# Sample tokens of the linear-attention layer: answers in four column tiles, state updates from values spread through DRAM

## The reference, cut to what matters

```python
def gla_chunk_step(S, inp):
    q, k, v, g = inp
    ...
    o = jnp.einsum('bhij,bjhv->bihv', attn, v) + jnp.einsum('bihk,bhkv->bihv', q * jnp.exp(bcum), S)
    b_last = bcum[:, -1]
    k_dec = k * jnp.exp(b_last[:, None] - bcum)
    S = jnp.exp(b_last)[..., None] * S + jnp.einsum('bjhk,bjhv->bhkv', k_dec, v)
    return S, o
```

## Time and profile before

| | |
|---|---|
| median of 3 runs | 1551.72 us (1551.42 to 1552.45) |
| the profiled execution | 1551.42 us, span 1549.7 us |
| TensorE busy | 1447.2 us (93%) |
| VectorE busy | 1175.9 us (76%) |
| ScalarE busy | 822.4 us (53%) |
| GpSimd busy | 248.7 us (16%) |
| mean granted TensorE clock | 0.981 |
| DMA | 243.11 MB, mean 157 GB/s |
| step 0 of heads 0, 1, 2, 3 | near 84 to 109, 173 to 194, 247 to 266 and 329 to 359 us |

### The profile page before, as it was taken

The page is one execution under the profiler, slowest core; times in us unless marked ns, Lnnn a source line. Parts: engine busy times, 40 slices in busy tenths (PEclk is TensorE's granted clock), DMA queues, the critical chain, the costliest instruction groups (busy, mean ns, idle before and its releaser), DMA issues. The chain is left out here.

```text
span 1549.7 us, 31393 instructions
## 1 busy us (share of the span) xinstructions
PE 1447.2 (93%) x11610; PEld 1195.0 (77%) x11610; DVE 1175.9 (76%) x2595; ACT 822.4 (53%) x1837; POOL 248.7 (16%) x438
## 2 busy tenths in 40 slices
PE   6999999799999979899999999989999999999985
PEld 5979787666788858898888888767787777777754
DVE  4555587856786887968977898986879787587775
ACT  4735353446465544546655765653657364655451
POOL 5010113101231200012111112120003110000012
PEclk8999999999999999999999999999999999999998
DMA  6455455335476542547854764843585664554541
GB/s 190 132 155 148 129 168 151 112 114 171 120 205 191 160 122 71 150 122 182 253 145 121 237 191 140 240 140 94 167 247 143 189 183 144 175 150 150 175 137 61
DMA packets 283778, 243.11 MB, mean 157 GB/s; under 512 B 32856, under 2 KB 251036, under 8 KB 283468
## 3 DMA queue, kind: packets, MB, share of 16 engines
q1 hardware_dynamic: 273708, 208.28, 45.6%
q0 software_dynamic: 9920, 32.84, 7.9%
HBM read 180.40 MB, written 64.97 MB: 158 GB/s over the span
## 5 line engine op out<-in xcount | busy, mean ns | idle before, releaser
L1447 PE MATMUL bank<-h,w 128*128 128x268 f32 (+1 forms) x4752 | 835.3, 330 | 22.5 <-ACT w L857 15.8
L1447 PEld LDWEIGHTS bank<-h,w 128*128 128x128 f32 x4752 | 699.4, 191 | 102.1 <-issue 28.4
L873 DVE TENSOR_TENSOR w<-w_raw,w 128x1024 fp32r<-128x1024 f32 x132 | 160.9, 1219 | 35.5 <-ACT w L857 34.9
L842 PE MATMUL bank<-s_w_out,s_yt_hi 128*128 128x512 f32 (+2 forms) x544 | 169.8, 402 | 3.8 <-DVE s_ys L2532 3.8
L857 ACT ACTIVATE w<-w_raw 128x1024 fp32r<-128x1024 f32 x132 | 138.7, 1051 | 8.1 <-DMA w_raw<-in_ssd_w_in_dram 8.1
L1525 DVE SCALAR_TENSOR_TENSOR conv<-before_conv,cw,conv 128x260 f32<-128x260 f32 (+2 forms) x216 | 125.3, 580 | 4.2
L842 PEld LDWEIGHTS bank<-s_w_out,s_yt_hi 128*128 128x128 f32 (+2 forms) x544 | 97.1, 182 | 30.8 <-issue 4.4
L842 PE MATMUL bank<-g_w_out,g_ot_hi 128*128 128x512 f32 (+2 forms) x288 | 97.0, 426 | 1.6 <-DVE g_ot_lo L2073 1.3
L842 PE MATMUL bank<-s_w_out,s_yt_lo 128*128 128x512 f32 x240 | 95.6, 398 | 0.0
L2616 ACT ACTIVATE s_yt_hi<-bank 128x512 fp32r<-128x512 f32 (+1 forms) x36 | 20.1, 557 | 126.5 <-PE bank L2607 126.4
L2319 ACT ACTIVATE s_decay<-s_decay,t_ac 128x128 f32<-128x128 f32 (+1 forms) x288 | 85.4, 379 | 1.2
(11 more groups left out here) (256 smaller groups left out, 2503.4 us busy)
## 6 DMA issues: line engine op xcount, KB each, us to landing
w_raw<-in_ssd_w_in_dram SPq DMA_DIRECT2D x80, 512.0 KB, 4.3
w_raw<-in_gla_w_in_dram SPq DMA_DIRECT2D x48, 512.0 KB, 4.3
s_decay<-kept_acd SPq DMA_DIRECT2D x32, 512.0 KB, 6.2
w_raw<-in_ssd_w_out_dram SPq DMA_DIRECT2D x30, 512.0 KB, 4.0
g_chunk<-kept_gq SPq DMA_DIRECT2D x32, 448.0 KB, 4.9
s_chunk<-kept_sq SPq DMA_DIRECT2D x32, 384.0 KB, 4.8
kept_sq<-stage SPq DMA_DIRECT2D x80, 134.0 KB, 4.3
kept_sq<-stage SPq DMA_DIRECT2D x40, 256.0 KB, 4.7
```

Source lines behind the costliest of these rows:

```text
L842: last = pe.matmul(bank[0:r, :], yt[a][:, k, 0:r], wo[:, b, 512 * half:512 * half + 512], start=(k + a + b == 0), stop=(k == tiles - 1 and ...
L873: dve.tensor_tensor(self.part(i, 1), self.raw(i), hi, ALU.subtract).then_inc(self.w_lo, 1)
L1447: last = pe.matmul(bank[:, 0:n], w[:, p.tile % 2, a, k, :], h[:, b, k, c:c + n], start=(i == 0), stop=(i == len(terms) - 1))
```

## The change

The answers: `g_q_masked` gets 32 columns per sample, and each answer product writes one column tile, 32 partitions of the second half of bank `O`, with sample c in tile c mod 4. Tasks 0 and 2 do nothing on TensorE, ScalarE and VectorE; task 1 handles four samples and task 3 the other four, each with four products. ScalarE copies the bank's half to `g_answers`, and one product with a stack of four identities (`g_near_masks`, last slot) adds the four tiles into the step's output, ahead of the attention's own product.

The new states: SP stores the 8 rows of values to DRAM (`store_values`, behind ScalarE's turned values) and loads them back spread over all 128 partitions, 1 MB (`load_values`, behind a wait for the store's landing). ScalarE scales each state by its decay in place, behind its answer, and VectorE adds value times key. The outer products, `g_k_masked` and VectorE's `dve_keys` go; ScalarE turns the meta tokens' keys with a scale that clears the samples' rows. GpSimd's task stays as it was, four times a head. Some semaphores of the size computation are merged.

```diff
         gla = [("distance", 1), ("keys", 0), ("levels", 0), ("decay", 1), ("turn", -1), ("fill", 0.5), ("load", 2),
...
-               ("fill", 0.5), ("lows",), ("fill", 0.5), ("weight", 1, 0), ("r_square", -1), ("r_out", -2),
-               ("fill", 0.5), ("lows",)]
+               ("fill", 0.5), ("lows",), ("fill", 0.5), ("v_out", 1), ("weight", 1, 0), ("r_square", -1), ("r_out", -2),
+               ("fill", 0.5), ("lows",), ("v_in", 1)]
...
-                 (0, ("scale", 0))]
+                 (0, ("scale", 0)), (0, ("v_out", 0)), (0, ("v_in", 0))]
...
-                            for i in range(4):
+                            for i in (1, 3):
+                                tasks.append(("sample", L, u, i - 1))
                                 tasks.append(("sample", L, u, i))
-                                tasks.append(("fill", at[0]))
+                                tasks.append(("fill", 2 * at[0]))
...
+    def store_values(self, sp, u):
+        e = ev(u, 0)
+        sp.wait_ge(self.vr_turned, e + 1)
+        sp.dma_start(self.d["v_rows"][u], self.t["vr"][0:NS, e % 2, 0:HV]).then_inc(self.v_moved, 16)
+
+    def load_values(self, sp, u):
+        sp.wait_ge(self.v_moved, 32 * u + 16)
+        if u:
+            sp.wait_ge(self.ss_new, NS * u)
+        sp.dma_start(self.t["vb"][:, :, :], self.d["v_rows"][u].unsqueeze(0).to_broadcast([P, NS, HV])).then_inc(
+            self.v_moved, 16)
...
+        for q in (4 * u + i - 1, 4 * u + i):
+            pe.wait_ge(self.ss_in[q % SAMPLES], 16 * (q // SAMPLES + 1))
+        for j in range(4):
+            c = 2 * (i - 1) + j
+            last = pe.matmul(self.O[SUB * j:SUB * (j + 1), HV:2 * HV], t["qm"][:, c * SUB:(c + 1) * SUB],
+                             t["ss"][:, (4 * u + c // 2) % SAMPLES, c % 2, :], start=(i == 1), stop=(i == 3))
         last.then_inc(self.ss_prod, 1)
...
+    def act_sample(self, act, u, i):
+        t, e = self.t, ev(u, 0)
+        if i % 2 == 0:
+            return
+        act.wait_ge(self.ss_prod, 2 * u + i // 2 + 1)
+        if i == 3:
+            act.activation(t["part"][:, :], self.O[:, HV:2 * HV], ACT.Copy).then_inc(self.ss_kept, 1)
+        for q in (i - 1, i):
+            for b in range(2):
+                st = t["ss"][:, (4 * u + q) % SAMPLES, b, :]
+                last = act.activation(st, st, ACT.Copy, scale=t["eb"][:, e % 2, 2 * q + b:2 * q + b + 1])
+            last.then_inc(self.ss_kept, 1)
...
+        dve.wait_ge(self.v_moved, 32 * (u + 1))
+        dve.wait_ge(self.k_ready0, 2 * (u + 1))
+        for q in (i - 1, i):
+            dve.wait_ge(self.ss_kept, self.kept_count(u, q))
+            for b in range(2):
+                c, st = 2 * q + b, t["ss"][:, (4 * u + q) % SAMPLES, b, :]
+                dve.scalar_tensor_tensor(out=st, in0=t["vb"][:, c, :], scalar=t["kd0"][:, c:c + 1], in1=st,
+                                         op0=ALU.mult, op1=ALU.add).then_inc(self.ss_new, 1)
...
+        if s == 0:
+            pe.wait_ge(self.ss_kept, 5 * u + 3)
+            pe.matmul(self.O[0:n, 0:HV], self.t["near"][:, 5, 0:n], self.t["part"][:, :], start=True, stop=False)
```

More of the change, by code:

```diff
@@ L559, in _ @@
                 ssd.load_first_z(sp, *at)
+            elif name == "v_out":
+                gla.store_values(sp, *at)
+            elif name == "v_in":
+                gla.load_values(sp, *at)
         gla.all_saved(sp)
@@ L617, in _ @@
                 ssd.act_inputs(act, *at[1:])
-            elif name == "sample" and at[0] == 1:
-                ssd.act_sample(act, *at[1:])
+            elif name == "sample":
+                layers[at[0]].act_sample(act, *at[1:])
             elif name == "square":
@@ L1704, in prepare @@
         t, consts = self.t, self.consts
-        mask, mask0, rowsel = t["mask"], t["mask0"], t["rowsel"]
+        mask, mask0, late = t["mask"], t["mask0"], t["late"]
         for li, h in enumerate(gla_levels(1)[0]):
@@ L1708, in prepare @@
         pool.memset(mask0[:, :, :], 0.0).then_inc(consts, 1)
-        pool.memset(rowsel[:, NS:NS + 1], 1.0).then_inc(consts, 1)
-        pool.tensor_copy(rowsel[:, 0:NS], self.m["ident"][0:C0, 0:NS]).then_inc(consts, 1)
-        n = 10
+        pool.memset(late[:, :], 1.0).then_inc(consts, 1)
+        n = 9
         pool.wait_ge(consts, n)
@@ L1789, in dve_distance @@
         if e == 0:
-            dve.wait_ge(self.zeros, 6)
+            dve.wait_ge(self.zeros, 7)
             dve.wait_ge(self.consts, self.CONSTS)
@@ L1967, in pe_sample @@
     def pe_sample(self, pe, u, i):
-        t, n = self.t, C0
-        if i == 0:
+        t = self.t
+        if i % 2 == 0:
+            return
+        if i == 1:
             self.output_free(pe, ev(u, 0))
             pe.wait_ge(self.qm_ready, u + 1)
-            pe.wait_ge(self.km_ready, u + 1)
-        i += 4 * u
-        pe.wait_ge(self.ss_in[i % SAMPLES], 16 * (i // SAMPLES + 1))
-        for b in range(2):
-            c = 2 * (i % 4) + b
-            pe.matmul(self.O[0:n, 0:HV], t["qm"][:, c * C0:(c + 1) * C0], t["ss"][:, i % SAMPLES, b, :],
-                      start=(c == 0), stop=False)
@@ L1979, in pe_sample @@
-        if i % 4 < 2:
-            pe.wait_ge(self.attn, ev(u, 0) + 1)
-        else:
-            pe.wait_ge(self.ss_new, 2 * (i - 1))
-        for b in range(2):
-            c = 2 * (i % 4) + b
-            last = pe.matmul(self.L[i % 2][:, b * HV:(b + 1) * HV], t["km"][:, c, :], self.values(u, 0),
-                             start=True, stop=True)
-        last.then_inc(self.ss_prod, 1)
-    def dve_sample(self, dve, u, i):
-        t, e = self.t, ev(u, 0)
-        i += 4 * u
-        dve.wait_ge(self.ss_prod, i + 1)
-        for b in range(2):
-            c = 2 * (i % 4) + b
-            dve.scalar_tensor_tensor(out=t["ss"][:, i % SAMPLES, b, :], in0=t["ss"][:, i % SAMPLES, b, :],
-                                     scalar=t["eb"][:, e % 2, c:c + 1], in1=self.L[i % 2][:, b * HV:(b + 1) * HV],
-                                     op0=ALU.mult, op1=ALU.add).then_inc(self.ss_new, 1)
+        for q in (4 * u + i - 1, 4 * u + i):
+            pe.wait_ge(self.ss_in[q % SAMPLES], 16 * (q // SAMPLES + 1))
@@ L2004, in pe_state @@
         if s == 0:
-            pe.matmul(self.TB[:, P:P + HV], t["km"][:, NS, :], v, start=True, stop=True).then_inc(self.s_prod, 1)
+            pe.wait_ge(self.k_turned, e + 1)
+            pe.matmul(self.TB[:, P:P + HV], t["kt"][0:n, :], v, start=True, stop=True).then_inc(self.s_prod, 1)
         else:
             self.output_free(pe, e)
-            pe.wait_ge(self.k_turned, sum(1 for _, q in EVENTS[:e + 1] if q))
+            pe.wait_ge(self.k_turned, e + 1)
             pe.wait_ge(self.s_new, e)
@@ L2079, in pe_products @@
         pe.wait_ge(self.attn, min(e + 2, len(EVENTS)))
-        if e + 1 < len(EVENTS) and EVENTS[e + 1][1] == 0:
-            pe.wait_ge(self.ss_new, 2 * 4 * (EVENTS[e + 1][0] + 1))
         for half in range(2):
```

70 lines of the change are left out of this document (36 added, 34 removed).

## The result

The changed kernel takes 1563.58 us (median of five runs, 1559.24 to 1565.44); the kernel before, in the same comparison, 1551.72 (five runs, 1551.20 to 1557.38), 11.9 us less. The ratio is 1.0059, with an interval of 1.0041 to 1.0078: slower. The profiled execution took 1564.17 us, its span is 1562.5. Against the profiled execution of before that is 12.8 us more.

What follows compares the result with a forecast made beforehand. TensorE, busy for 93% of the span, was taken as the bound. To the profiled 1551.42 us came 1.8 (later state products), 2.1 (adding products) and 6.0 (clock): 1561.3, stated as 1561.5, range 1548.5 to 1571.

Steps and rivals of the forecast that it cites:

- Products: TensorE, four heads: sets at 0.6 us each replace 8.1 us of products a head; 25.6 us less work in all.
- Waits of 5 to 9 us: TensorE idles 5 to 9 us before each head's second set, until the fourth sample state's load lands.
- a sign of being wrong: A second set on TensorE that starts without a wait, or waits under 3 us.
- From update to issue: From VectorE's first state update to GpSimd's issue of the fourth state's load: 1.95 us.
- So the values decide: Head 0: values are spread at 93.1 us, after the first set's pair is scaled at 92.4, so the copy sets the start.
- 6.1 for 1 MB: SP's load of the spread values: 6.1 us for 1 MB, from 4.3 for 512 KB and 0.9 per 256 KB.
- That is 1.5 us lost each time: Half clock on TensorE behind the wait at each of four second sets: 1.5 us each, 6.0 in all.
- (c): Rival: the four column tiles on TensorE run one after another, about 6 us more: 1567.5 us; chance 0.10.
- (b): Rival: the fourth state's load is no obstacle, all of TensorE's saving comes through: 1523 us; chance 0.04.
- (a): Rival: values spread before the first set's pair is scaled, 3.4 us per state load, three gaps' clock: 1546 us; chance 0.14.
- (d): Rival: the values' copy takes 8.9 us, 2.8 more in heads 0 to 2: 1570 us; chance 0.14.
- (e): Rival: gaps partly absorbed where TensorE later waits for VectorE, or the clock holds: 1551 to 1556 us; chance 0.13.

Runs made afterwards that it cites:

- experiment 1: The changed kernel with all four sample states of a head loaded before the head begins: 1528.13 us, ratio 0.9826 to the kernel before.
- experiment 5: The changed kernel unedited, run once more on a second chip: 1562.84 us, ratio 1.0064 to the kernel before.
- experiment 7: The kernel of experiment 1 with all eight answer products of a head in one column tile instead of four: 1537.13 us, ratio 0.9901.
- experiment 3: The changed kernel with 6, 12, 17 and 15 unread 256-column products in front of the second sets of heads 0 to 3: 1553.16 us, ratio 0.9987.
- experiment 6: The changed kernel with all fill products moved between the two sets, loads left as they are: 1551.36 us, ratio 0.9990.

## Why the prediction was right

1561.5 us was forecast and 1563.58 measured, by the mechanism that it named: the products saved turn into waits before each second set, released by the fourth state's load, with the lower clock behind them. That the number was met to 2 us is in part luck, since two of its terms were wrong in opposite directions. Point by point:

- **Products.** A set was priced at 0.6 us and takes 0.64. Of the 25.6 us forecast to go off TensorE's queue experiment 1 shows 24.0, in busy time; its span is 24.1 us shorter.
- **Waits of 5 to 9 us.** They are 3.28, 6.71, 9.11 and 8.22. Head 0 lies outside, near the 3 us that was named as a sign of being wrong: its load took 3.3 us where 5.4 was taken from before, and the copy didn't decide there.
- **From update to issue**, 1.95 us: 1.91 to 1.97.
- **The copy.** "So the values decide" was wrong in heads 0 and 1, and so was the sign that VectorE's first update would be released by the spread values in heads 0 to 2. The store of 8 KB was priced at 2.3 us from one of 268 KB; in heads 0 and 1 the load behind it was issued 1.31 and 1.32 us after the store's own issue, while in heads 2 and 3 it was 3.18 and 3.01. The load of 1 MB let VectorE go 4.86 us after its issue in head 2 (255.87 to 260.73); the step "6.1 for 1 MB" was over-sized. The Trainium skill's fit (DMA: Bandwidth & Descriptors, Anatomy of one DMA), given there for transfers that GpSimd issues while this one is SP's, makes it 4.4 us, an estimate from that page that I had set aside; the measured 4.86 lies nearer to it than to mine. The error made the forecast 2.6 us too dear: head 0's update came at 91.95 us for 93.1, and head 1's 2.64 us behind its first set, 181.1 in times of before, for 182.6. In head 2, where the copy mattered, SP came to it late, as foreseen.
- **ScalarE.** Four scalings of 128x256 take 1.7 us together, 0.42 each; 0.4 was taken.
- **The clock** is the mis-sized term. "That is 1.5 us lost each time" came from one stretch of 3.1 us; the stretches measured 4.2 to 12.8 us, and 14.9 us were lost in place of 6.0, in another execution 8.6. No term stood for the 1.6 us at 317.5.

The terms by head, as what each adds to TensorE's lateness at the state product (forecast with 1.5 us of clock in each, and with the adding product of the head before):

| head | forecast, us | measured, us | what differs |
|---|---|---|---|
| 0 | +0.3 | -2.0 | load 3.3 for 5.4; copy in time; clock 1.5 more |
| 1 | +2.0 | +0.35 | load 4.3 for 5.0; copy in time |
| 2 | +3.8 | +7.95 | half clock of head 1 runs on to 199 us, 4.4 |
| 3 | +3.2 | +5.1 | 1.6 of clock at 317.5, ahead of its samples; from its first set on 2.85 for 2.7 |
| rest | +0.6 | +1.4 | |
| sum | +9.9 | +12.8 | |

So errors of opposite sign met. Without the clock heads 0 and 1 were priced 6 us too dear (2.3 and 1.65 by the table, and 2.0 us of clock beyond the forecast lie ahead of their state products), 2.8 of it in the two loads (3.3 for 5.4, 4.3 for 5.0) and 2.6 in the copy. The clock was 8.9 us too cheap in the four stretches and 1.6 at 317.5. Head 3's load (4.1 for 5.7) gives 1.6 back: 9.9 - 6.0 + 8.9 + 1.6 - 1.6 = 12.8, as near as counting by the half allows. That they cancel so well belongs to the profiled execution: in that of experiment 5 the clock cost 6.3 us less in the stretches. In head 2 alone, from its first set on, the chain was right to 0.2 us: the first set stood 2.8 us later than before (254.78 to 252.00), the state product was forecast at 265.7 + 2.8 + 1.5 = 270.0 and stood at 270.19.

Of the rivals, (c), serial tiles, is ruled out by experiment 7. (b), all of the saving through, is what the change gives once its loads are early: 1523 was worked out, 1528.13 measured, 1524.7 by the ratio on the prediction's chip. (a) was right that the loads are quicker and that the copy is in time in heads 0 and 1, and wrong that three gaps cost 4.5 us of clock. (d), a copy of 8.9 us, is ruled out by the 4.86 us in head 2. Of (e), waits elsewhere are 2.2 us shorter, but the clock didn't hold. What makes the length of the low clock differ from head to head stays open; no run here separates it.

## What to carry to other kernels

When steps of a ring are merged, count what stands ahead of each load: a ring of four that is filled three ahead asks for its fourth buffer only behind the first's release, and the work that used to lie between is what hid it. Price a wait on TensorE twice, as the idle time and as the time at the lower clock behind it, which here was from a quarter to nearly as much again. Before such a change is dropped as slower, move the loads: here that turned +0.6% into -1.7%.

## What the runs showed of the hardware that was not expected

- Behind idle times of 3.3 to 9.1 us TensorE stayed at a granted clock of 0.50 for 4.2 to 12.8 us while busy without a break, and for how long didn't follow the length of the idle time: 12.8 us behind 6.71, 4.2 behind 9.11. In a second execution with the same waits the 12.8 were some 4. In experiments 3 and 6 it was 10.0 us behind 1.84 and at least 10.2 behind 5.77 (180.8 to 191.0).
- Nor did the length of a short wait tell whether the clock fell. In experiment 3 it fell behind 1.84 us and held behind 1.28 and 0.83; in experiment 6 it fell behind 1.07. Behind the wait of 2.62 or 2.63 us for ScalarE's weights in front of head 3, 24 products took 5.80 or 5.81 us in eight of the ten profiles here, at full clock in the one of before, and 7.38 and 7.34 in those of the changed kernel and of experiment 3.
- Four products of 32 columns of weights in four column tiles take 0.64 us, in one tile 1.91: 3.0 times as long. In experiment 1 the whole products behind a tiled set start 0.57 us after the set's start (171.42 to 171.99), so no row shows a loss at the change from tiled to whole products.
- A store of 8 KB and the wait for its landing passed in 1.31 and 1.32 us on SP's queue in heads 0 and 1, and in 3.18 and 3.01 us in heads 2 and 3.
